# Blocks of matmuls of zeros in front of waits of the matmul engine, in a two-part network of 256 tokens

## The reference, cut to what matters

```python
# first block
x = x + 0.5 * swiglu(rmsnorm(x), w_in, w_out)          # ffn0, ffn1, ffn2, ffn3
x = x + hgrn2_mixer(rmsnorm(x), ...)                   # hgrn: 8 heads
gate = sigmoid(rmsnorm(x) @ ple_w_gate)
x = x + gate * (p @ ple_w_in)                          # ple0, ple1
k_nope, k_rope, v = mla_shared_kv(x, ...)              # kv
x = x + mla_mixer(rmsnorm(x), k_nope, k_rope, v, ...)  # dq (queries' latent) and mla: 16 heads
x = rmsnorm(x)                                         # final
# second block
x = x + even_mixer(rms_norm(x), ...)                   # even: stick-breaking attention and pooling
x = x + odd_mixer(rms_norm(x), ...)                    # odd: gated linear attention
x = x + conv_ffn(rms_norm(x), ...)                     # conv0, conv1
```

## Time and profile before

| what | value |
|---|---|
| time, median of 3 runs | 2038.83 us (2037.73 to 2039.31) |
| time of the profiled execution | 2033.37 us |
| its span, first to last instruction | 2031.5 us |
| busy: PE, DVE, ACT, POOL | 93%, 58%, 48%, 26% |
| mean granted TensorE clock | 0.964 of 2.4 GHz |

### The profile page before, as it was taken

One profiled execution on the slowest core, in us unless ns is written; L12 is line 12 of the kernel. 1 busy time (PEld: TensorE's weight loads), 2 busy tenths in 40 slices (PEclk: granted clock), 3 DMA queues, 4 the chain that ended last, 5 costly groups with the idle time before them and its releaser, 6 DMA issues.

```text
span 2031.5 us, 37971 instructions
## 1 busy us (share of the span) xinstructions
PE 1886.8 (93%) x14978; PEld 1839.2 (91%) x14978; DVE 1182.1 (58%) x1708; ACT 971.8 (48%) x1108; POOL 538.0 (26%) x427
## 2 busy tenths in 40 slices
PE   7999799889998799989998999879789999989999
PEld 7999789879998799987897999878789999989999
DVE  6654778755553555544555555463367774337776
ACT  5443667653444743352334444453355555545554
POOL 2002546610005300054552000564310016570001
PEclk9999999989998899998999999889899998999999
DMA  6556323335543455532333555242225452343553
GB/s 224 198 186 223 111 103 108 119 108 184 185 163 98 149 203 180 183 119 78 124 117 111 191 186 174 88 157 83 104 107 186 184 195 97 110 166 130 183 180 116
DMA packets 47025, 300.05 MB, mean 148 GB/s; under 512 B 5216, under 2 KB 5600, under 8 KB 18800
## 3 DMA queue, kind: packets, MB, share of 16 engines
q1 hardware_dynamic: 46960, 299.15, 41.6%
HBM read 298.08 MB, written 1.05 MB: 147 GB/s over the span
## 4 chain that ended last, share of the span: by engine, by line
PE 67%; issue 16%; POOL 7%; DVE 7%; ACT 3%; DMA 1%; POOLq 0%; SPq 0%; ACTq 0%; DVEq 0%
PE wk L328 12%; PE wk L330 12%; PE wk L329 12%; POOL w_lo L2146 7%; PE acc L328 6%; PE acc L330 6%; PE acc L329 6%; PE wk L339 2%; PE wk L340 2%; PE wk L338 2%; DVE x_lo L516 1%; ACT w_hi L282 1%; DVE sumsq L530 1%; PE wk L1383 1%; PE wk L1381 1%
## 5 line engine op out<-in xcount | busy, mean ns | idle before, releaser
L2146 POOL TENSOR_TENSOR w_lo<-raw,w_hi 128x512 fp32r<-128x512 f32 (+2 forms) x421 | 537.2, 1308 | 1478.7 <-ACT w_hi L282 1478.7
L328 PE MATMUL wk<-x_hi,w_hi 128*128 128x256 f32 x2688 | 777.0, 289 | 45.1 <-DVE x_lo L516 22.7
L282 ACT ACTIVATE w_hi<-raw 128x2048 fp32r<-128x2048 f32 (+6 forms) x313 | 538.0, 1726 | 524.0 <-PE wk L330 393.3
L329 PE MATMUL wk<-x_lo,w_hi 128*128 128x256 f32 x2688 | 768.6, 286 | 0.0
L330 PE MATMUL wk<-x_hi,w_lo 128*128 128x256 f32 x2688 | 768.5, 286 | 0.0
L328 PEld LDWEIGHTS wk<-x_hi,w_hi 128*128 128x128 f32 x2688 | 524.5, 195 | 51.9 <-DVE x_lo L516 24.5
L329 PEld LDWEIGHTS wk<-x_lo,w_hi 128*128 128x128 f32 x2688 | 524.3, 195 | 0.4
L330 PEld LDWEIGHTS wk<-x_hi,w_lo 128*128 128x128 f32 x2688 | 523.6, 195 | 0.0
L302 DVE TENSOR_TENSOR w_lo<-raw,w_hi 128x2048 fp32r<-128x2048 f32 x180 | 411.8, 2290 | 160.3 <-ACT w_hi L282 160.3
L328 PE MATMUL acc<-h_hi,w_hi 128*128 128x256 f32 x1376 | 393.1, 286 | 27.3 <-DVE h_lo L1084 10.3
L329 PE MATMUL acc<-h_lo,w_hi 128*128 128x256 f32 x1376 | 388.5, 282 | 0.0
(11 more groups left out here) (285 smaller groups left out, 2028.3 us busy)
## 6 DMA issues: line engine op xcount, KB each, us to landing
raw<-w_ffn_loop SPq DMA_DIRECT2D x120, 1024.0 KB, 4.8
raw<-w_conv_loop SPq DMA_DIRECT2D x60, 1024.0 KB, 4.8
raw<-w_hgrn_loop SPq DMA_DIRECT2D x18, 896.0 KB, 4.5
raw<-w_mla_loop SPq DMA_DIRECT2D x18, 768.0 KB, 4.2
raw<-w_ple SPq DMA_DIRECT2D x24, 448.0 KB, 3.2
raw<-w_odd_loop SPq DMA_DIRECT2D x12, 704.0 KB, 4.0
raw<-w_ffn_first SPq DMA_DIRECT2D x6, 1024.0 KB, 4.8
raw<-w_even_loop SPq DMA_DIRECT2D x6, 1024.0 KB, 4.7
```

The costliest lines, as they stand in the source:

```text
L282: nc.scalar.activation(w_hi[slot][:, 0:seg.T * P], raw[slot][:, 0:seg.T * P], ACT.Copy).then_inc(S("hi_ready"), 1)
L328: nc.tensor.matmul(dst, hi, a_hi, start=start, stop=False, skip_group_check=True)
L329: nc.tensor.matmul(dst, hi, a_lo, start=False, stop=False, skip_group_check=True)
L2146: last = nc.gpsimd.tensor_tensor(w_lo[slot][:, a:b], raw[slot][:, a:b], w_hi[slot][:, a:b].bitcast(F32), ALU.subtract)
```

## The change

A new function `keep_warm(n)` issues n matmuls with zeros as both operands, which add zero to bank 0 of `acc`. It is called with fixed numbers in front of waits of the matmul engine: four places in hgrn, one at the head of ffn2, two in each ple phase, two each in kv, dq and mla, five in even and one in odd. Loops whose bodies hold a call under a condition on the first or last head execute it once. No other engine's instructions change.

```diff
--- before.py
+++ after.py
@@ -360,6 +360,12 @@
             for b in range(4):
                 nc.tensor.matmul(acc[:, b, :], zero[:, 0:P], zero[:, :], start=True, stop=False, skip_group_check=True)
 
+        def keep_warm(n):
+
+            for _ in range(n):
+                last = nc.tensor.matmul(acc[:, 0, :], zero[:, 0:P], zero[:, :], start=False, stop=False, skip_group_check=True)
+            return last
+
         def dve_add_acc(v, name, factor, last_seg):
 
             def update(b):
@@ -571,6 +577,9 @@
         def pe_ffn(pe, name):
             first, loop, last = ffn_segs(name)
             n0 = ffn_index[name] * NJ
+
+            if name == "ffn2":
+                keep_warm(14)
 
             def up(seg, i, j, opening=False):
 
@@ -872,6 +881,7 @@
                     if has_last:
                         HG_V_GATHER.after(pe, i - 1, "across")
                     else:
+                        keep_warm(13)
                         HG_V_PREP.after(pe, i, "q")
                     use_tiles(pe, *seg, 0, f_q[:8])
                 if has_last:
@@ -894,6 +904,8 @@
                     HG_V_GATHER.after(pe, i - 1, "across")
                 HG_P_SCORES.done(nc.tensor.matmul(wk[:, 0, 0:P], kt[:, LEVELS, 0:P], qt[:, LEVELS, P:SEQ], start=True, stop=True,
                                                   skip_group_check=True), "across")
+                if not has_next:
+                    keep_warm(19)
                 HG_V_GATHER.after(pe, i, "a3")
                 round_(i, 1)
                 if has_last:
@@ -902,6 +914,8 @@
                         use_tiles(pe, *seg, 32, out_tiles(1))
                     else:
                         use_tiles(pe, out0, 0, 0, out_tiles(1))
+                if not has_last:
+                    keep_warm(22)
                 HG_V_GATHER.after(pe, i, "b3")
                 HG_V_VALUES.after(pe, i, "v")
                 nc.tensor.matmul(wk[:, 2, 0:SEQ], hg_v[:, 0:P], hg_st[:, 0:SEQ], start=True, stop=False, skip_group_check=True)
@@ -918,6 +932,7 @@
                 body(r + 1)
             body(A_HEADS - 1, has_next=False)
             mean(A_HEADS - 1)
+            keep_warm(29)
             HG_V_OUT.after(pe, A_HEADS - 1, "lo")
             last_outputs(pe, out1, 1)
 
@@ -1167,9 +1182,11 @@
                     for k in range(KD):
                         x_lo_ready(pe, name, k)
                         use_tiles(pe, seg, 0, 2 * k, hs[2 * k:2 * k + 2])
+                    keep_warm(14)
                     pe.wait_ge(S("ple_p_lo"), p0 + 1)
                     use_tiles(pe, seg, 0, 16, hs[16:])
                     pe_mean(pe, name)
+                    keep_warm(8)
                 else:
                     use_tiles(pe, seg, i, 0, hs)
 
@@ -1223,8 +1240,11 @@
             outs = [x_tiles(wk[:, n // 2, n % 2 * SEQ:n % 2 * SEQ + SEQ], n % 2 == 0) for n in range(nk)]
             if name == "kv":
                 outs.append(x_tiles(wk[:, 1, 0:SEQ], True))
+            if name == "kv":
+                keep_warm(14)
             opening_tiles(pe, name, (seg, 0), side_by_side(*outs), len(outs))
             pe_mean(pe, name)
+            keep_warm(18 if name == "kv" else 8)
             if name == "dq":
                 pe.wait_ge(S("rstd_ready"), 2 * norm_index[name] + 1)
                 pe_mla_keys(pe, 0, 0)
@@ -1233,6 +1253,8 @@
                 last = nc.tensor.matmul(wk[:, 0, 0:SEQ], const(mean), la_sq[:, k * SEQ:k * SEQ + SEQ], start=(k == 0), stop=(k == nk - 1),
                                         skip_group_check=True)
             LA_PE.done(last, "mean")
+            if name == "dq":
+                keep_warm(17)
             if name == "kv":
                 pe.wait_ge(S("kr_scaled"), 1)
                 nc.tensor.matmul(wk[:, 3, 0:SEQ], const("rotate"), kr_in, start=True, stop=True, skip_group_check=True).then_inc(S("kr_rotated"), 1)
@@ -1405,6 +1427,8 @@
                 if has_next:
                     project(i + 1)
                     ML_V_PROJ.after(pe, i + 1, "v_tmp")
+                else:
+                    keep_warm(24)
                 transpose(i)
                 if has_next:
                     rotate(i + 1)
@@ -1422,6 +1446,7 @@
             with pe.Fori(0, loop.n) as r:
                 body(r + 1)
             body(B_PAIRS - 1, has_next=False)
+            keep_warm(9)
             ML_V_OUT.after(pe, B_PAIRS - 1, "lo")
             use_tiles(pe, out1, 0, 0, out_tiles(2)[:KD])
             last_outputs(pe, out1, 2)
@@ -1627,19 +1652,25 @@
                     pe.wait_ge(S("pool_w_landed"), 16)
                 EV_P_O.done(nc.tensor.matmul(wk[:, 0, SEQ:512], pool_sb[:, i, :], ev_pool, start=True, stop=True, skip_group_check=True), "pool")
 
+            keep_warm(22)
             opening_tiles(pe, "even", (proj0, 0), qk_tiles, 2)
             use_tiles(pe, proj0, 0, 16, v_tiles[:8])
             pe_mean(pe, "even")
             use_tiles(pe, proj0, 0, 24, v_tiles[8:])
             pe_clear_acc(pe, "even")
             mean(0)
+            keep_warm(9)
             for i in range(SB_PAIRS):
                 seg = proj_place("even", i + 1)
                 z(i)
                 if i + 1 < SB_PAIRS:
                     EV_V_OUT.after(pe, i - 1, "pool")
                     use_tiles(pe, *seg, 0, qk_tiles)
+                if i + 1 == SB_PAIRS:
+                    keep_warm(25)
                 later(i)
+                if i + 1 == SB_PAIRS:
+                    keep_warm(9)
                 if i + 1 < SB_PAIRS:
                     mean(i + 1)
                     EV_V_VALUES.after(pe, i, "xb")
@@ -1652,6 +1683,7 @@
                     else:
                         use_tiles(pe, out0, 0, 0, out_tiles(2))
                 pool(i)
+            keep_warm(12)
             EV_V_OUT.after(pe, SB_PAIRS - 1, "lo")
             use_tiles(pe, out1, 0, 0, out_tiles(2)[:KD])
             last_outputs(pe, out1, 2)
@@ -1900,6 +1932,7 @@
                     else:
                         use_tiles(pe, out0, 0, 0, out_tiles(2))
             mean_logit(GLA_HEADS)
+            keep_warm(28)
             OD_V_OUT.after(pe, GLA_HEADS - 1, "lo")
             use_tiles(pe, out1, 0, 0, out_tiles(2)[:KD])
             last_outputs(pe, out1, 2)
```

## The result

The changed kernel takes 2009.57 us (median of 4 runs, 2006.58 to 2010.27) against 2038.28 us (4 runs): ratio 0.9856, 95% interval 0.9844 to 0.9869. The forecast was 2010 us, between 2000 and 2027. The profiled execution of the changed kernel took 2009.02 us with a span of 2007.2 us; that of before 2033.37 and 2031.5. So the two spans differ by 24.3 us, the medians by 28.7.

The account below looks back on a forecast made before the run. The matmul engine's work plus waits bound the kernel, about 7% at half clock. Sixteen stretches' ceiling of 36.6 us, less 1.1, 1.0, 2.3, 1.3 and 2.3, gave 28.6; from the median 2038.83, 2010 us, range 2000 to 2027.

Parts of the forecast that it names:

- the 19: Block of 19 zero matmuls in the last HGRN head, behind the across matmul, where the wait is 2.04 us.
- The zeros rival: Matmuls of zeros do not hold the clock, so blocks run low and overrun: 2058 us, chance 0.10.
- The price of the low clock: From the PLE projections, 0.219 us each low and 0.1187 high: 0.458 of busy time in a low stretch is lost.
- even's opening: Stretch at 1335.89: VectorE's eight x_lo set the pace at any clock, so all of its gain, 2.3 us, is deducted.
- 1366.61: Low stretch, 3.42 us busy: VectorE's final-norm work releases the engine, so 0.3 us stays and 1.3 is deducted.
- the PLE phases: Stretches at 632.75 and 1298.35: GpSimd's units about keep even with the matmul engine; 0.5 us deducted for each.
- The seam after HGRN: Stretch at 421.12: the FFN behind needs x_lo, then rstd, so 1.4 of 2.5 us stays; 1.1 deducted.
- The overrun: In the last HGRN head the block of 19 outlasts its wait and starts round b 2.3 us late, on the path.
- the six stretches without a block: Low-clock stretches after waits with no zeros in front, 30.74 us in all; about 31 us would still be low.
- Hidden time: Rival: waits for x_lo or w_lo take 15.2 us at PLE phases and seams to FFNs; 2025 us, chance 0.13.
- A low clock met by a block: Rival: blocks starting at low clock overrun further, another wait proves too short; 8 us lost, 2018 us, chance 0.12.
- More goes: Rival: the 10.24 us low stretch at 922.88 may vanish too, 4.7 us more; 2005 us, chance 0.08.

Follow-up runs that it names:

- the experiment without the 22: The changed kernel with the block of 22 zero matmuls ahead of even's opening left out: 2009.23 us, ratio 0.9854 to the kernel before.
- the further blocks: The changed kernel with its block of 19 moved ahead of round a, and blocks of 8, 5, 16, 10, 11 and 5 at further waits: 1999.37 us.

## Why the prediction was right

**The mechanism** is the one it named. Zeros hold the clock: it stayed up through the block of 6.94 us and, but for its first 0.4 us, through the one of 4.78. The waits with a block shrank to between 0.3 and 1.2 us (under 1.1 was forecast), and to nothing where the 19 stand. The Trainium skill ("TensorE: Matmul & The Clock Gate", section "What's actually happening") has the gate set by "how busy the PE has been recently", and the trace agrees: matmuls whose data is all zero count. The zeros rival is out: it wanted 2058 us.

**The price of the low clock**, 0.458 of the busy time, carried over to most stretches. Of the seventeen steps of the table that have a term, thirteen lie within 0.6 us of it.

**The deductions**: even's opening gained nothing (the experiment without the 22), and its waits for x_lo behind the first one grew from 1.4 to 3.2 us, as the prediction said they would; 1366.61 gave nothing for 0.3; the PLE phases gave 4.4 and 3.5 for 4.3 and 3.8. The seam after HGRN gave 1.8 for 1.4. HGRN's first head gave 2.3 for 3.1: round a started behind a wait of its own of 0.46 us for VectorE's keys, which the prediction did not deduct; the other 0.3 us are not accounted for.

**The overrun** was 2.8 us for 2.3. A slower round a (3.75 us for 3.41, its low stretch fell earlier) put the start of the block 0.3 us further back, at 405.39, and it ended at 410.0, 0.2 us behind 405.39 + 19 x 0.233, its first zeros being at the low clock.

**What it mis-sized** is the assumption that the six stretches without a block stay as they were. In the profiled execution they did not: a new one from 931.44 cost 2.5 us, the wait before even's first later grew from 2.90 to 4.40 us, because VectorE's final norm sets its end, and its stretch from 3.42 to 6.83 us (1.2 us); odd's shrank (0.9 us back). "About 31 us would still be low" was 40.94 us. Part of this belongs to the execution and not to the kernel: in the two further ones the stretch from 931.44 is missing, odd's did not shrink (6.83 us in both), and one has the 10.24 us in even's opening. From the profiled execution the sum gave 2004.8 us; it took 2009.0.

**Why the median fits all the same:** the profiled execution of before was a quick one, 4.9 us under its median, that of after 0.6 us under. The sum was 4.3 us too large and the difference of the medians 4.4 us larger than that of the profiles. The hit to half a microsecond is chance; the agreement to some 4 us is not. What makes most executions of before lie between 2032 and 2044 us was not settled; the mean granted clock does not sort them (0.962 at 2032.2 and at 2039.9).

**The rivals.** Hidden time: the waits for w_lo rose from 5.7 to 6.9 us. Those for x_lo fell from 22.7 to 14.0, but mostly because blocks now fill two of them and the kernel's first was shorter; what is left beside these three rose from 1.7 to 3.6 us, nearly all in even's opening, which was deducted. So some 1.2 us can have been hidden beyond the terms, for the rival's 15.2. A low clock met by a block: only the first 0.4 us of the 19. More goes: not in this kernel, whose 10.24 us stretch stayed, but it is what the further blocks bring, 2011.2 to 1999.4 us.

## What to carry to other kernels

A wait of the matmul engine costs its own length and, where the clock falls, part of what runs behind it at half the clock. The granted clock laid beside the waits shows both. Matmuls of zeros into an open accumulator fill a wait for nothing while they end before the operand, are paid beyond it unless a later wait takes them in, and are worth nothing where another engine paces what follows. Their numbers fit one set of waits: after each change read again which waits have grown, which are bare, and which block overruns. Profile a kernel more than once before a single low stretch is put down to a change.

## What the runs showed that was not expected

- The same wait of 3.28 us lowered the clock in one kernel and not in another, 1.69 us started 10.24 us of it, and 2.65 us none. In executions of one kernel the same wait of 1.39 us was followed by 6.82 us of low clock once and by none twice, and once 10.24 us came 10 us behind the last wait of over 0.4 us. The prediction's "every one begins during or just after a wait" holds for the trace of before and not in general.
- A zero matmul of 128x512 takes 0.43 us from start to start at the low clock. The rows below, from the block of 7 at the head of ffn2 in the kernel with half blocks, show it: three take 0.43 us more than the last two of them; 0.438 us was the bound that the prediction took. At the high clock it takes (6.94 - 0.39)/28 = 0.234 us. The Trainium skill ("TensorE: Matmul & The Clock Gate", section "Wait — 56ns, not 53.3ns?") has 426.7 ns cold, which agrees, and 215.7 ns warm, which does not.

```profile
680.02 1.05 PE L366 MATMUL acc<-zero 128*128 128x512 f32 x2
679.60 1.48 PE L366 MATMUL acc<-zero 128*128 128x512 f32 x3
```
